# Stream update of the second block in wide vector operations, squares summed there, gate-and-up tiles over seven PSUM banks

## The reference

```
h = rmsnorm(x, norm_mix[i]);  x = x + mixer(h)
h = rmsnorm(x, norm_ffn[i]);  x = x + (silu(h @ w_gate) * (h @ w_up)) @ w_out
```

```
h = h + 0.5 * rmsnorm(swiglu(rmsnorm(h, g[0]), ...), g[1])
h = h + rmsnorm(mix(rmsnorm(h, g[2])), g[3])
h = h + 0.5 * rmsnorm(swiglu(rmsnorm(h, g[4]), ...), g[5])
```

## Time and profile before

| what | value |
|---|---|
| median of 3 runs | 1949.22 us (1944.98 to 1959.04) |
| the profiled execution | 1958.64 us, span 1956.8 us |
| PE busy | 1870.8 us (96%) |
| DVE busy | 1270.1 us (65%) |
| ACT busy | 918.7 us (47%) |
| POOL busy | 161.6 us (8%) |
| mean granted clock of TensorE | 0.951 of full speed (2.4 GHz) |
| chain that ended last | PE 86%, DVE 8%, ACT 2%, DMA 2% |

### The profile page before, as it was taken

One profiled execution on the slowest core, in us unless ns is written; L12 is line 12 of the kernel. 1 busy time (PEld: TensorE's weight loads), 2 busy tenths in 40 slices (PEclk: granted clock), 3 DMA queues, 4 the chain that ended last, 5 costly groups with the idle time before them and its releaser, 6 DMA issues.

```text
span 1956.8 us, 33004 instructions
## 1 busy us (share of the span) xinstructions
PE 1870.8 (96%) x13432; PEld 1723.9 (88%) x13432; DVE 1270.1 (65%) x2132; ACT 918.7 (47%) x1581; POOL 161.6 (8%) x204
## 2 busy tenths in 40 slices
PE   6989998999999999999988999999999998999997
PEld 6979996887569998999978878999899996589997
DVE  6867668764467766766565338665776657657664
ACT  7545444442455454544454235444544443445452
POOL 1001005100000001000020022000200011020001
PEclk9999999996799999999998889999999998789999
DMA  4215555530015556555533223555355551125553
GB/s 152 76 41 183 185 187 200 181 134 20 1 44 183 184 189 202 178 175 173 194 108 108 65 76 130 172 173 192 129 187 186 191 183 54 33 87 188 188 194 120
DMA packets 76038, 276.35 MB, mean 141 GB/s; under 512 B 8496, under 2 KB 9520, under 8 KB 75760
## 3 DMA queue, kind: packets, MB, share of 16 engines
q1 hardware_dynamic: 75168, 270.57, 41.3%
q0 software_dynamic: 288, 2.30, 0.4%
q10 hardware_dynamic: 432, 1.38, 0.2%
HBM read 273.16 MB, written 1.05 MB: 140 GB/s over the span
## 4 chain that ended last, share of the span: by engine, by line
PE 86%; DVE 8%; ACT 2%; DMA 2%; issue 1%; POOL 0%; SPq 0%; DVEq 0%; POOLq 0%; ACTq 0%
PE acc L1555 57%; PE acc L1551 5%; PE mix L245 3%; PE mix L1555 2%; PE acc L1552 2%; DMA arrived<-in_w 2%; DVE wl L1794 2%; DVE y L1820 2%; PE acc L632 1%; PE acc L1624 1%; DVE xl L1806 1%; PE acc L1597 1%; PE mix L656 1%; PE acc L1575 1%; PE acc L1047 1%
## 5 line engine op out<-in xcount | busy, mean ns | idle before, releaser
L1794 DVE TENSOR_TENSOR wl<-arrived,wh 128x1024 fp32r<-128x1024 f32 x514 | 641.2, 1248 | 396.7 <-ACT wh L1670 384.6
L1670 ACT ACTIVATE wh<-arrived 128x1024 fp32r<-128x1024 f32 x514 | 541.4, 1058 | 589.0 <-DMA arrived<-in_w 588.5
L1555 PE MATMUL acc<-xh,wh 128*128 128x256 f32 (+1 forms) x2376 | 678.1, 285 | 2.6 <-DVEq L1856 2.2
L1555 PE MATMUL acc<-xh,wl 128*128 128x256 f32 (+1 forms) x2376 | 675.9, 284 | 0.0
L1555 PE MATMUL acc<-xl,wh 128*128 128x256 f32 (+1 forms) x2376 | 675.5, 284 | 0.0
L1555 PEld LDWEIGHTS acc<-xh,wh 128*128 128x128 f32 x2376 | 450.1, 189 | 8.6 <-issue 7.8
L1555 PEld LDWEIGHTS acc<-xh,wl 128*128 128x128 f32 x2376 | 450.5, 190 | 0.0
L1555 PEld LDWEIGHTS acc<-xl,wh 128*128 128x128 f32 x2376 | 448.5, 189 | 0.3
L1555 PE MATMUL acc<-hx,wh 128*128 128x256 f32 (+1 forms) x1664 | 304.1, 284 | 0.0
L1555 PEld LDWEIGHTS acc<-hx,wh 128*128 128x128 f32 x1664 | 258.9, 189 | 0.8 <-issue 0.8
L1555 PE MATMUL acc<-hx,wl 128*128 128x256 f32 (+1 forms) x832 | 236.9, 285 | 0.0
(11 more groups left out here) (387 smaller groups left out, 2225.6 us busy)
## 6 DMA issues: line engine op xcount, KB each, us to landing
arrived<-in_w SPq DMA_DIRECT2D x514, 512.0 KB, 3.3
scr<-in_cmp_w POOLq DMA_DIRECT2D x1, 2048.0 KB, 9.0
x<-in_x ACTq DMA_DIRECT2D x2, 544.0 KB, 8.1
out<-x SPq DMA_DIRECT2D x8, 128.0 KB, 1.7
par<-in_par ACTq DMA_DIRECT2D x1, 259.0 KB, 4.1
scr<-in_positions POOLq DMA_DIRECT2D x1, 128.0 KB, 7.2
scr<-in_cmp_w POOLq DMA_DIRECT2D x1, 32.0 KB, 9.6
scr<-in_w_gate POOLq DMA_DIRECT2D x1, 32.0 KB, 2.7
```

The lines of the kernel that those rows point to most:

```text
L1555: ins = nc.tensor.matmul(bank(name, t)[:, 0:L - c], w_part[:, h.slot, w], v_part[:, k, c:], start=(k == 0 and w_part is wh and v_part is h ...
L1670: nc.scalar.activation(wh[:, h.slot, :], raw(h.slot), ACT.Copy).then_inc(w_hi, 1)
L1794: nc.vector.tensor_tensor(wl[:, h.slot, :], raw(h.slot), wh[:, h.slot, :].bitcast(F32), ALU.subtract).then_inc(w_lo, 1)
```

## The change

DVE alone updates x in the second block. It works on the k tiles in five groups, `GROUPS` = (0), (1), (2, 3), (4, 5), (6, 7): one scaling and one addition for each group, so the last three are operations of twice the width. POOL's additions go. DVE then makes the low parts (at u = 7 only those of the shared keys), then does its split of the next weight piece, and then sums all eight tiles of squares in three operations of 4, 2 and 1 tiles' width; at u = 7 the low parts for ffn4 come behind that. POOL keeps the sums for the post norms and for the first block. The mean of these five norms is one product in place of two, and in `opening` it stands behind all tiles of the group, not behind the second. On ACT, `ahead(b)` of the last output tile moves behind the root, the high parts and the squares. Gate-and-up tiles of all feed-forward networks take the banks `(mix + acc)[t % 7]`, and the waits for a free bank are computed from the order in which the tiles use the banks (`free_at`).

```diff
+GROUPS = ((0, 1), (1, 2), (2, 4), (4, 6), (6, 8))
...
         def bank(name, t):
+            if name.startswith("ffn") and name.endswith("_a"):
+                return (mix + acc)[t % 7]
...
+        free_at = []
+        _last = {}
+        for _name, _n in STAGES:
+            for _t in range(_n // KF_PARTS if _name.endswith("_b") else _n):
+                _bank = [b is bank(_name, _t) for b in mix + acc].index(True)
+                free_at.append(_last.get(_bank, 0))
+                _last[_bank] = TILE[_name] + _t + 1
+
+        def bank_free(pe, name, t):
+
+            if free_at[TILE[name] + t]:
+                pe.wait_ge(acc_used, free_at[TILE[name] + t])
+
+        def stream_new(eng, u, k):
+
+            if u < 5:
+                eng.wait_ge(x_new, 8 * (u - 1) + k + 1)
+            else:
+                eng.wait_ge(x_sum, len(GROUPS) * (u - 5) + [n for n, (f, e) in enumerate(GROUPS) if f <= k < e][0] + 1)
+
+        SUMMED_BY_DVE = [norm_of(u) for u in range(5, upto)]
...
-            def post_update(u):
-
-                norm_sum(norm_of(u, True), c0(u))
-
-                def add(k):
-                    pool.wait_ge(t_new, 8 * (u - 5) + k + 1)
-                    pool.tensor_tensor(x[:, k, c0(u):], x[:, k, c0(u):], y[:, k, c0(u):], ALU.add).then_inc(x_new[0], 1)
-
-                for k in range(0, KD, 2):
-                    add(k)
-                if u < upto:
-                    norm_sum(norm_of(u), c0(u))
...
                 if u >= 5:
-                    post_update(u)
+                    norm_sum(norm_of(u, True), c0(u))
...
                     ins.then_inc(used, 1)
-                    if norm is not None and (name, t) == group[1]:
-                        mean(norm_of(norm), c0(norm))
+                if norm is not None:
+                    mean(norm_of(norm), c0(norm))
...
                 mean_of = (ones4 if halved(v) else ones)[:]
+                if v in SUMMED_BY_DVE:
+                    nc.tensor.matmul(stat[:, 0:L - c], mean_of, sumsq[:, c:], start=True, stop=True).then_inc(mean_ok, 1)
+                    return
...
                     nc.scalar.activation(sq[:, m, c0(u):], bank(name, m)[:, 0:L - c0(u)], ACT.Square).then_inc(sq_new, 1)
-                    ahead(b)
+                    if m < KD - 1:
+                        ahead(b)
...
                         for k in range(KD // 2, KD):
                             squares(x, norm_of(u), k, c0(u))
-                    if u < 5:
-                        ahead(b)
+                    ahead(b)
...
+                def scaled(n):
+                    f, e = GROUPS[n]
+                    nc.vector.tensor_tensor(y[:, f:e, c:], y[:, f:e, c:], ry[:, c:].unsqueeze(1).to_broadcast([P, e - f, L - c]),
+                                            ALU.mult).then_inc(t_new, 1)
+
+                def add(n):
+                    f, e = GROUPS[n]
+                    dve.wait_ge(t_new, len(GROUPS) * (u - 5) + n + 1)
+                    nc.vector.tensor_tensor(x[:, f:e, c:], x[:, f:e, c:], y[:, f:e, c:], ALU.add).then_inc(x_sum, 1)
+
+                scaled(0)
+                scaled(1)
+                add(0)
+                add(1)
+                for n in range(2, len(GROUPS)):
+                    scaled(n)
+                    add(n)
                 if u == 7 and u < upto:
                     for k in range(KD):
                         kv_low(dve, k)
-                for k in range(KD):
-                    low_x(u, k)
+                else:
+                    for k in range(KD):
+                        low_x(u, k)
+                ahead(b)
+                if u < upto:
+                    norm_sum(norm_of(u), c)
+                if u == 7 and u < upto:
+                    for k in range(KD):
+                        low_x(u, k)
+
+            def norm_sum(v, c):
+
+                dve.wait_ge(sq_new, 8 * v + KD)
+                dve.wait_ge(mean_ok, v)
+                n = 2 * SUMMED_BY_DVE.index(v)
+                nc.vector.tensor_tensor(sq[:, 0:4, c:], sq[:, 0:4, c:], sq[:, 4:8, c:], ALU.add).then_inc(sum_part, 1)
+                dve.wait_ge(sum_part, n + 1)
+                nc.vector.tensor_tensor(sq[:, 0:2, c:], sq[:, 0:2, c:], sq[:, 2:4, c:], ALU.add).then_inc(sum_part, 1)
+                dve.wait_ge(sum_part, n + 2)
+                nc.vector.tensor_tensor(sumsq[:, c:], sq[:, 0, c:], sq[:, 1, c:], ALU.add).then_inc(sum_ok, 1)
```

More of the change, by code:

```diff
@@ L179, in build @@
         w_hi, w_lo, used, acc_used = sem("w_hi"), sem("w_lo"), sem("used"), sem("acc_used")
[L180 removed]
+        x_new, x_sum, sum_part = sem("x_new"), sem("x_sum"), sem("sum_part")
         x_hi, x_lo = sem("x_hi"), sem("x_lo")
@@ L1483, in _ @@
             for k in range(KD):
-                sp.wait_ge(x_new[k % 2], updated(upto, k))
+                stream_new(sp, upto, k)
                 sp.dma_start(out[k], x[:, k, META:]).then_inc(out_ok, 16)
@@ L1538, in _, with half @@
             pe.wait_ge(const_ok, 7)
-            def half(h, q, name, t, part, hi, lo, c, kt, wait):
+            def half(h, name, t, part, hi, lo, c, kt, wait):
                 pe.wait_ge(w_lo, h.n + 1)
-                if part == 0 and q >= 4:
-                    pe.wait_ge(acc_used, q - (1 if name == "gla_r" else 3))
+                if part == 0:
+                    bank_free(pe, name, t)
                 ks = range(part * KD, min(kt, part * KD + KD))
@@ L1565, in gemm @@
                     for part in range(parts):
-                        half(Half(BASE[name] + t * parts + part), TILE[name] + t, name, t, part, hi, lo, c, kt,
+                        half(Half(BASE[name] + t * parts + part), name, t, part, hi, lo, c, kt,
                              wait if t == 0 else None)
@@ L1587, in opening @@
                     pe.wait_ge(w_lo, BASE[name] + t + 1)
-                    if TILE[name] + t >= 4:
-                        pe.wait_ge(acc_used, TILE[name] + t - 3)
+                    bank_free(pe, name, t)
                     for k in range(KD):
@@ L1679, in high_x @@
                 if u:
-                    act.wait_ge(x_new[k % 2], updated(u, k))
+                    stream_new(act, u, k)
                 else:
@@ L1817, in post_norm @@
                 rms(norm_of(u, True), c, ry)
-                def scaled(k):
-                    nc.vector.tensor_tensor(y[:, k, c:], y[:, k, c:], ry[:, c:], ALU.mult).then_inc(t_new, 1)
-                def add(k):
-                    if k % 2:
-                        dve.wait_ge(t_new, 8 * (u - 5) + k + 1)
-                        nc.vector.tensor_tensor(x[:, k, c:], x[:, k, c:], y[:, k, c:], ALU.add).then_inc(x_new[1], 1)
-                for k in range(KD):
-                    scaled(k)
-                    if k:
-                        add(k - 1)
-                add(KD - 1)
-                ahead(b)
+                def scaled(n):
[13 more added lines that the diff above has]
+                    add(n)
                 if u == 7 and u < upto:
@@ L1853, in two @@
                         dve.wait_ge(used, b + 1)
-                        nc.vector.tensor_tensor(tg[:, t, c:], bank(name, 2 * t)[:, 0:L - c], rx[:, c:], ALU.mult).then_inc(f_g, 1)
+                        nc.vector.tensor_tensor(tg[:, t, c:], bank(name, 4 * i + 2 * t)[:, 0:L - c], rx[:, c:], ALU.mult).then_inc(f_g, 1)
                         dve.wait_ge(f_g, n)
@@ L1862, in two @@
                         dve.wait_ge(used, b + 2)
-                        nc.vector.tensor_tensor(tu[:, t, c:], bank(name, 2 * t + 1)[:, 0:L - c], rx[:, c:],
+                        nc.vector.tensor_tensor(tu[:, t, c:], bank(name, 4 * i + 2 * t + 1)[:, 0:L - c], rx[:, c:],
                                                 ALU.mult).then_inc(acc_used, 1)
@@ L1890, in tail @@
                         step(nc.vector.tensor_tensor(x[:, m, META:], x[:, m, META:], bank(name, m)[:, SEQ:2 * SEQ], ALU.add))
-                    nc.vector.tensor_tensor(x[:, m, META:], x[:, m, META:], bank(name, m)[:, 0:SEQ], ALU.add).then_inc(x_new[m % 2], 1)
-                    dve.wait_ge(x_new[m % 2], updated(u, m))
+                    nc.vector.tensor_tensor(x[:, m, META:], x[:, m, META:], bank(name, m)[:, 0:SEQ], ALU.add).then_inc(x_new, 1)
+                    dve.wait_ge(x_new, 8 * (u - 1) + m + 1)
                 else:
```

6 lines of the change are left out of this document (1 added, 5 removed).

## The result

The changed kernel took **1943.8 us**, median of 20 runs (1938.5 to 1954.8), against 1955.4 for the kernel before in the same session, also 20 runs (1943.5 to 1965.6): ratio 0.9938, interval 0.9918 to 0.9957. Over all timed runs of this study the means are 1956.8 ± 0.5 (107 runs) and 1944.5 ± 0.8 (38 runs; ± is the standard error), a gain of 12.4 ± 0.9 us, or 0.6%. The forecast was 18.3. So it is faster, by two thirds of the forecast, and within 1%. Against the predicted 1931 the time is 12.8 us higher: 6.2 because the kernel before itself came out at 1955.4 instead of the 1949.2 of the three runs shown, the rest because the gain by these two medians is 11.6 and not 18.3.

A forecast was written before the change was run, and what follows sets the result against it. PE was taken as the bound, busy 96% of the span, so only five openings and the tail could gain: 20.6 us, less 2.3 for the clock, is 18.3; 1949.2 - 18.3 = 1931 us, range 1921 to 1944.

The forecast's parts named there:

- Tile 5 of ffn3: Feed-forward opening: bank wait goes, a new 1.3 us wait for low weights replaces it; starts at 18.95, gains 5.3 us.
- GLA's entry: PE resumes at 19.5 instead of 23.1 us behind the first scaling, pausing 4.9 instead of 2.5; 4.2 us gained.
- From it I take the clock: Longer pauses at gla_lr, kv and swa_q bring the low clock: 2.3 us off the gain, bounds 0 and three times 1.7.
- theory C: Experiments' theory, no chance given: low clock comes and goes in GLA's own pauses and takes the gain back there.
- Theory E: Experiments' theory, no chance given: GLA's stretch is chance, no share of the miss assignable; the entry's 3.6 us do arrive.
- D: Experiments' theory, no chance given: something in GLA other than the clock has a fixed end.
- Rival 1: Openings: the cover holds and the clock does not fall; gain 20.6 up to 27 us, 1922 to 1929; chance 0.24.
- Rival 2: Five openings: the wait moves to the mean, low clock behind each pause; gain 5 to 14 us, 1935 to 1944; chance 0.20.
- Rival 3: Slower: low clock behind the new pauses lasts into the matmul-bound bodies; 1950 to 1970 us; chance 0.04.
- Rival 4: The change does nothing, DVE's chain work being only reordered; within 3 us; chance 0.02.
- POOL's price: Openings before the change: about 5.4 us of POOL's 9.3 us is lost to DVE, from first scaling to last low part.
- late split of the weights at kv: ACT's split behind the squares: PE waits 3.2 us before the mean; kv gains only 0.5 us, root included.

The follow-up runs named there:

- before_fill: The kernel before with 10 filler matmuls on constants in PE's pause at GLA's entry; 1962.1 us (one run).

## Why the prediction was wrong in size, and right in all steps but one

**Right.** The root is 0.04 us behind the mean (1389.53 + 0.62 to 1390.19). Wide scaling 0.72. Low parts 9.0 behind the scaling. Tile 5 of ffn3 at 19.07 (18.95), of ffn5 at 18.2 (17.9), with the new waits of 1.3 and 1.4 us. GLA's entry at 19.55 (19.5) behind a pause of 4.80 (4.8). ffn4's second tile at 24.15 (24.2), swa at 13.5 (13.1). Tail: the last addition ends 5.4 us behind the scaling (5.5). With the same steps read from both traces the sum before the clock is 19.6 us, where I had 20.6: 3.56, 5.13, -0.45, 3.87, 3.47 and 0.95 in the order of the prediction's list, and 3.09 for the roots. (At kv the prediction gave 3.1 us to a tile of ffn4, whose 24 matmuls of 256 columns take 2.9; the second tile began at 23.7 before, not 23.9.)

**The step that failed** is "From it I take the clock": 1.2, 0.6 and 0.5 us, "together 2.3". What stands in its place is 19.6 - 12.4 = 7.2 us; that is a remainder between steps of one pair of traces and the timed gain, not a reading. The size was wrong and so was the reasoning. I priced the low clock per new pause, and let the gain from the old ones stay: the openings did go from 0.81 to 0.92 up to 0.92 to 1.00, which frees 16.1 - 4.8 = 11.3 us at half clock. But the run's total stayed at 197 us. Within one kernel, over its runs, a us at half clock goes with 0.43 us of time (a matmul-bound stretch would lose 0.5), so 11.3 come to 4.9 to 5.7 us given back, most of the 7.2; 1.5 to 2.3 us stay open. The bounds for this term ended at 5.1, so even they did not hold it. Why the total stays when the openings lose their share is not shown.

**Where it came back.** Two places can be named. In the swa stretch the opening held 5.9 us at half clock before and 1.2 after, yet the whole stretch held 47 us in both, as a mean of three executions (44.6 to 48.0 before, 44.6 to 47.7 after), and its gain was 0.85 us short. In GLA the three changed executions held 55 us against 47, and the 4.2 - 1.2 - 0.15 = 2.85 us forecast there did not show in the means; but at the same time at half clock they are there, and the difference of 8 us is within the spread. The changed entry fixes one part of it: 5.57 us for the six products in every execution, against 3.20, 5.22 and 4.20. The slow opening behind gla_out (0.72 for 10.8 us instead of 0.83 for 9.6) is no effect of the change: the third execution of the changed kernel has 9.6 there, and before_fill, with the kernel before's update, 10.8. So theory C holds in part: GLA's length follows its time at half clock, and fillers shorten that in both kernels. Theory E holds in part as well, since the gain missing in GLA's ledger line is within the chance of three executions. And the fillers did not uncover a larger gain of the change, which at equal clock is 12.9 us with them or without. D falls: GLA has no fixed end.

**The rivals.** Rival 1 (up to 27) fell; the openings did get most of their clock back, but the run did not. Rival 2 named the right family, low clock behind pauses, and its 5 to 14 us hold the result; its mechanism did not come true, since the mean came no later in four-tile openings and the wide operations were on the line. Its prices also add up to 14 to 19 us where it says 5 to 15, so its range holding the result is luck. The rule that the prediction cites from the Trainium skill, "TensorE: Matmul & The Clock Gate", Part 1, is that activity lifts the throttle. That every pause, however short, is followed by half speed was the prediction's own reading of it. The 10.4 us worked out so, an estimate at 1.7 us for each of six pauses, is nearer to 12.4 than my 18.3 is, but by luck too: behind the new waits of 1.3 and 1.4 us ffn3's and ffn5's whole stretches ran without any time at half clock, and of the pauses looked at here only GLA's entry has the low clock right behind its pause (0.50 over 5.5 us). I had set the reading aside on one window, the 1.00 behind ffn3's 1.1 us. That window was right for ffn3 and ffn5, and said nothing of GLA, whose stretch I had not read for its clock. Rival 3 (slower) did not come: the feed-forward stretches gained what they should. Rival 4 fell by ffn3 alone.

**The rest.** POOL's price: over the low parts DVE lost 2.6 us (5.97 - 3.39) while POOL was busy for 4.2, a little over half, as in the rows' 5.4 of 9.3. "SBUF — State Buffer" of the Trainium skill, section on the two sides of SBUF, has the two lock each other out entirely; by that all 4.2 us would be lost, which this trace does not bear out. The wide operations were costed rightly and are worth nothing; the price of the late split of the weights at kv was right.

## What to carry to other kernels

Where part of a run is at the low clock, take nothing for the clock that a stage gets back until the clock of the whole run moves: here the openings gained 11 us of full clock and the run none. Compare two kernels at the same time at half clock, run by run: that turned 12.4 ± 0.9 and 16.1 ± 1.8 us into 12.9 and 12.8. Look where the matrix engine pauses elsewhere, and fill those pauses with products on constants in the same build; in GLA that was worth 9 us on the changed kernel and 6 on the one before, where the one mended order at kv was worth 3. And before giving a stretch a share of the miss, profile both kernels three times: one stretch here moved by 8 us without an edit.

## What the runs showed that I had not expected

The granted clock stayed at a mean of 0.949 to 0.950 for the whole run, though the openings held 11 us less of half clock. Six short products took 5.57 us behind every pause of 4.8 us, 3.20 to 5.22 behind pauses of 2.0 to 2.8, and 2.93 with the pause filled. One pair of scaling and add follows the next after 0.83 us at 272 columns and after 1.39 at 544, so double width saves 0.27 us in 1.66. Runs of the same kernel differ by 21 us (1933.5 to 1954.8), and the run's time follows its time at half clock at 0.43 us for each.
